# The order of the on-chip tensors in SBUF changed: operand tiles, weight homes, WORK and BIG first, landing buffers and residual behind

## What is computed

```python
for layer in range(2):                       # first block
    u = rmsnorm(h, norm_g[layer, 0])
    m = even_mixer(u, ...) if layer == 0 else nsa_mixer(u, ...)   # u @ w_in, attention-like work, @ w_out
    h = h + rmsnorm(m, norm_g[layer, 1])
    u = rmsnorm(h, norm_g[layer, 2])
    gate, up = split(u @ ffn_w_gu[layer])    # 2048 -> 2 x 5632
    h = h + rmsnorm((silu(gate) * up) @ ffn_w_down[layer], norm_g[layer, 3])
for layer in range(2):                       # second block, smaller mixers: 2048 -> 2048, 512 -> 2048, then a final rmsnorm
    ...
```

## The kernel before

| tensor | before | after |
|---|---|---|
| `H`, the residual | 16512 to 32896 | 198912 to 215296 |
| `UTH` | 32896 to 49280 | 16512 to 32896 |
| `UTL` | 49280 to 65664 | 32896 to 49280 |
| `RAW0` to `RAW3` | 65664 to 82048 | 182528 to 198912 |
| `WH`, `WL` of homes 0 to 2 | 82048 to 106624 | 49280 to 73856 |
| `BIG` | 106624 to 172288 | 116864 to 182528 |
| `WORK` | 172288 to 215296 | 73856 to 116864 |
| `HTH` (in `BIG`) | 106624 to 151680 | 116864 to 161920 |
| `HTL1` (in `BIG`) | 151680 to 163968 | 161920 to 174208 |
| `HTL0` (in `WORK`) | 172288 to 205056 | 73856 to 106624 |
| extra homes 0 to 3 (in `WORK`) | 172288 to 205056 | 73856 to 106624 |
| extra homes 4 and 5 (in `BIG`) | 127360 to 140416 and 168064 to 172160 (`XL5`) | 137600 to 150656 and 178304 to 182400 (`XL5`) |
| `WC`, `MK`, `ONE`, `SM` and the small ones | from 215296 | the same |

## Time and profile before

### The profile page before, as it was taken

How to read it: one execution, slowest core, us unless ns; L and a number is a source line. 1 busy time by engine, 2 the same in 40 slices (tenths; PEclk the granted TensorE clock), 3 DMA queues, 4 the chain that set the end, 5 groups by cost and what they waited for, 6 DMA issues and landing times.

```text
span 2812.7 us, 33205 instructions
## 1 busy us (share of the span) xinstructions
PE 2787.0 (99%) x13548; PEld 2320.3 (82%) x13548; DVE 1578.5 (56%) x2212; ACT 1368.8 (49%) x2031; POOL 61.0 (2%) x83
## 2 busy tenths in 40 slices
PE   9999999999999999999999999999999999999998
PEld 7788888888888888888888888888888888887777
DVE  6665777755545454444644555654555544466666
ACT  6645454545444444333634544644444443356565
POOL 0000000000000000000010000000000000000002
PEclk9999999999999999999999999999999999999999
DMA  7855544665666666555655434666666655565444
GB/s 233 139 128 131 108 105 99 167 208 178 193 182 193 189 190 190 188 194 187 218 172 155 135 105 153 191 189 193 187 190 185 194 188 191 190 204 170 153 142 135
DMA packets 213497, 481.12 MB, mean 171 GB/s; under 512 B 15584, under 2 KB 16352, under 8 KB 212704
## 3 DMA queue, kind: packets, MB, share of 16 engines
q1 hardware_dynamic: 210848, 467.78, 56.9%
q0 software_dynamic: 2352, 11.17, 1.1%
q10 hardware_dynamic: 144, 0.05, 0.0%
HBM read 476.84 MB, written 2.10 MB: 170 GB/s over the span
## 4 chain that ended last, share of the span: by engine, by line
PE 90%; DVE 5%; ACT 2%; DMA 1%; issue 1%; POOL 0%; SPq 0%; ACTq 0%; POOLq 0%
PE PS L1105 19%; PE PS L1107 19%; PE PS L1106 19%; PE PS L1154 8%; PE PS L1153 8%; PE PS L1152 8%; DVE WL L2150 1%; DVE WORK L2309 1%; PE PS L1366 1%; ACT WH L1628 1%; PE PS L1269 1%; PE PS L1486 1%; PE PS L1184 1%; PE PS L1281 1%; PE PS L1282 1%
## 5 line engine op out<-in xcount | busy, mean ns | idle before, releaser
L2150 DVE TENSOR_TENSOR WL<-RAW,WH 128x1024 fp32r<-128x1024 f32 x826 | 1011.0, 1225 | 940.8 <-ACT WH L1628 939.1
L1628 ACT ACTIVATE WH<-RAW 128x1024 fp32r<-128x1024 f32 x830 | 874.8, 1055 | 841.6 <-PE PS L1107 526.9
L1105 PE MATMUL PS<-WH,UTH 128*128 128x512 f32 x2396 | 955.9, 399 | 3.9 <-DVE WL L2150 3.0
L1107 PE MATMUL PS<-WH,UTL 128*128 128x512 f32 x2396 | 935.1, 390 | 0.0
L1106 PE MATMUL PS<-WL,UTH 128*128 128x512 f32 x2396 | 934.0, 390 | 0.0
L1105 PEld LDWEIGHTS PS<-WH,UTH 128*128 128x128 f32 x2396 | 450.2, 188 | 99.3 <-issue 4.0
L1107 PEld LDWEIGHTS PS<-WH,UTL 128*128 128x128 f32 x2396 | 449.8, 188 | 97.3
L1106 PEld LDWEIGHTS PS<-WL,UTH 128*128 128x128 f32 x2396 | 450.6, 188 | 87.1
L1154 PE MATMUL PS<-WH,HTL 128*128 128x512 f32 x656 | 259.3, 395 | 0.0
L1153 PE MATMUL PS<-WL,HTH 128*128 128x512 f32 x656 | 258.8, 394 | 0.0
L1152 PE MATMUL PS<-WH,HTH 128*128 128x512 f32 x656 | 255.4, 389 | 0.0
(11 more groups left out here) (421 smaller groups left out, 2413.4 us busy)
## 6 DMA issues: line engine op xcount, KB each, us to landing
RAW<-in_ffn_w_gu SPq DMA_DIRECT2D x352, 512.0 KB, 4.3
RAW<-in_ffn_w_down SPq DMA_DIRECT2D x176, 512.0 KB, 4.5
RAW<-in_ab_w_in SPq DMA_DIRECT2D x128, 512.0 KB, 4.7
RAW<-in_nsa_w_in SPq DMA_DIRECT2D x80, 512.0 KB, 3.7
RAW<-in_w_in SPq DMA_DIRECT2D x64, 512.0 KB, 4.0
RAW<-in_ab_w_out SPq DMA_DIRECT2D x32, 512.0 KB, 4.6
RAW<-in_nsa_w_out SPq DMA_DIRECT2D x32, 512.0 KB, 4.2
RAW<-in_w_out SPq DMA_DIRECT2D x16, 512.0 KB, 4.4
```

The costliest lines, as they stand in the source:

```text
L1105: e.matmul(o, lh, wh[:, j], start=k + j == 0, stop=False)
L1107: x = e.matmul(o, ll, wh[:, j], start=False, stop=k + j == NKT - 1)
L1628: e.activation(wh, raw, ACTF.Copy).then_inc(*a_hi.inc(s))
L2150: e.tensor_tensor(wl, raw, wh.bitcast(F32), ALU.subtract).then_inc(*v_lo.inc(s))
```

## The change

The declarations in `build` stand in another order. No instruction, size, semaphore or loop is touched, and every engine has the same instructions in the same order as before. What moves is where each tensor lies (the table above). `WORK` and `BIG` also change places, and what is laid over them goes along.

```diff
-        H = sb("H", 2 * D)[:].rearrange("p (t n) -> p t n", t=2)
         UTH = sb("UTH", NKT * 256, F32R)[:].rearrange("p (k n) -> p k n", k=NKT)
         UTL = sb("UTL", NKT * 256, F32R)[:].rearrange("p (k n) -> p k n", k=NKT)
-        RAW = [sb(f"RAW{i}", SLOT)[:] for i in range(NRAW)]
         WHL = [(sb(f"WH{i}", SLOT, F32R)[:], sb(f"WL{i}", SLOT, F32R)[:]) for i in range(NW)]
+        work_at = -(-nc.sbuf_base // 32) * 32
+        WORK = sb("WORK", 10752)[:]
         big_at = -(-nc.sbuf_base // 32) * 32
         BIG = sb("BIG", 2 * CHUNKS_EVEN)[:]
-        work_at = -(-nc.sbuf_base // 32) * 32
-        WORK = sb("WORK", 10752)[:]
+        RAW = [sb(f"RAW{i}", SLOT)[:] for i in range(NRAW)]
+        H = sb("H", 2 * D)[:].rearrange("p (t n) -> p t n", t=2)
         GB = WORK[:, 8704:10752]
         room = [work_at + 4096 * i for i in range(8)] + [big_at + 4 * a for a in (5184, 6400, 7424, 15360)]
```

## The result

The changed kernel takes 2806.99 us (median of 8 runs, 2806.17 to 2814.97). The ratio to the kernel before is 0.9966, with a 95% interval of 0.9955 to 0.9977: 0.34% faster, 0.9 us under the forecast. The profiled execution has a span of 2804.4 us where it had 2812.7, 8.3 us less. The 0.9 us under the forecast are mostly not in the trace: the forecast put 2.9 us around the span, taken from the span of one execution and the median of others, and the profiled execution of the changed kernel, whose own time is known, has 1.8 us (2806.17 less 2804.4).

The account below looks back on a forecast made before the run. TensorE was taken to bound the kernel, by matmul count times spacing. -6.8 - 1.6 + 0.4 + 0.3 = -7.7 us on a 2812.7 us span, plus 2.9 us around it, gave 2807.9 us; range 2806.6 to 2809.6, widened 2 us below and to 2813 above.

Parts of the forecast that it names:

- a costly region: From about byte 172200 of a partition up, TensorE's reads cost more: 6.2 ns a matmul (moving), 13.2 ns a triple (stationary).
- What bounds the kernel: TensorE, busy 99% of the span, sets the time: the number of matmuls times their spacing.
- `HTL0`, 6.8 us: Feed-forward stages: moving `HTL0` from byte 172288 to 73856 saves 13.2 ns in each of 512 triples, 6.8 us off.
- The extra homes, 1.6 us: Extra homes 0 to 3 move down too: 432 matmuls at up to 6.2 ns, bounds 0 to 2.7 us, 1.6 us off.
- The end of `HTL1`, +0.4 us: Tiles k = 42 and 43 of `HTL1` move past about byte 172200: 32 triples at 13.2 ns, 0.4 us lost.
- `XL5`, +0.3 us: `XL5`, moving operand of 32 matmuls, moves up to byte 178304: 6.2 to 13.2 ns each, 0.3 us lost.
- The rival of no change: The cost hangs on which tensors are read in turn and returns with new neighbours: 2815.6 us; chance 0.15 within 0.2%.
- The slower rival: The bottom of memory, where `UTH` now lies, costs like the top: 2816 triples, 37.2 us more, 2845 us; chance 0.07.
- Landings and the copies of ScalarE and VectorE, 0: Loads landing in high buffers, and `RAW` read from there by ScalarE and VectorE, cost nothing; later landings could cost 2.2 us.

Follow-up runs that it names:

- `before_work128`: The kernel before, in its old order, with 128 bytes of unused space ahead of `WORK`, which then starts at byte 172416; 2805.58 us, ratio 0.9969.

## Why the prediction was right, and where it was wrong

The time lay in the forecast range, but the mechanism that the forecast rests on, a costly region, does not exist.

**What bounds the kernel: right.** Nothing moved but the spacing of TensorE, and the span followed its busy time.

**`HTL0`, 6.8 us: right in size, not in cause.** 512 triples went from 693.2 to 680.0 ns, and the count from the starts gives 6.8 us.

**The extra homes, 1.6 us: slightly too much.** They gave 1.2 us. In the open stretch the gain was in full, 3.96 to 3.85 us over 17 spacings; behind transposes and waits it was covered, as supposed, and more of them may stand there than I took; that was not counted.

**The end of `HTL1`, +0.4 us, and `XL5`, +0.3 us: wrong, both are nothing.** The step that failed is the reading of the cause: "somewhere at about byte 172200 of a partition a region begins from which TensorE's reads cost more, whichever operand it is". The rows were right, and so was the grouping of tensors into slow and quick; the property that I picked to tell them apart was one of two that fit. The address splits them at 172200, and so does the remainder by 256. The runs put the second in its place: fp32r matmuls cost 6 to 7 ns more when their operands differ in that remainder, in either order of the tensors. I held against a relation between operands that like spacings came with very different distances. Those distances, such as 118784 bytes, are all multiples of 256, and the 65664 bytes from `HTH` to `HTL0` are 256 x 256.5. (The prediction counts five extra tensors with the low spacing; the extra homes 4 and 5 are four.)

That the time was hit all the same was luck of the case: region and remainder agree on every term but the two small ones, and the errors (0.7 us of loss that did not come, 0.4 us of gain that did not) nearly cancel. For the kernel `before_work128` the prediction's reasoning would have said no change, and it would have missed all of it.

**The rival of no change.** It said that the cost may hang on which tensors are read in turn. As a form of the cause it was nearer than my own; its consequence, a like cost among the new neighbours, did not come, since the move happened to make all fp32r operands alike. The Trainium skill, page "SBUF — State Buffer", section "Who interferes with whom", was the page for that rival; the runs contradict the reading of it by which a place costs TensorE nothing (2804.4 against 2841.1 us of span by 128 bytes of two tensors).

**The slower rival.** `UTH` at the bottom costs nothing. That 37.2 us, its price for slow triples on `UTH`, is close to what `UTH` and `UTL` cost when they are unlike (36.7 us) is chance: it is made of 13.2 ns a triple in all 2816 triples, while the run has some 20 ns a triple where nothing interrupts (3 x 6.6) and much of it covered elsewhere. The run that has 13.2 ns a triple, with `UTL` alone, costs 27.3 us.

**Landings and the copies of ScalarE and VectorE, 0: right.** TensorE's waits stayed at 6.5 and 6.6 us, and the busy times of both engines moved by 0.6 us or less.

What stays open: why the remainder by 256 bytes matters, differences under 32 bytes, other data types, and what keeps the spacing from settling with an unlike `WL`.

## What to carry to other kernels

Where TensorE streams fp32r matmuls back to back, lay all their operands, stationary and moving, at the same remainder by 256 bytes, tensors laid over others included; a single pad of 128 bytes was worth 0.3% here, and two tensors 128 bytes off cost 1.3% (36.7 us of 2804.4). When a step in the spacing follows a tensor, list every property in which it differs from its neighbours (region, remainder, distance, buffer) before naming one, and look for a tensor on which two of them disagree, or make one with a pad. A change of declarations that seems to be about order may work by its remainders alone.

## What the runs showed of the hardware

- **The remainder by 256 bytes.** On fp32r operands with 512 moving columns the spacing is 226.7 ns with like remainders (0, 128, 160 and 192 tried) and 233.3 ns with unlike ones (32, 64 and 128 apart), at a granted clock of 1.00 in both. One unlike stationary tile slows two matmuls. An unlike `WL`, moving in one of three, costs 6 to 7 ns a triple in some stretches and 20 ns in most. Transposes of 128 columns, and the one fp32 matmul that was seen both ways, show no difference (272 and 274 to 275 ns). The Trainium skill, page "SBUF — State Buffer", section "Operand start alignment", calls the start address a question of "legality, not speed" and says that its own runs timed nothing; here it is one of speed.
- **A fall of the granted clock.** In the kernel with all operands at 160, and in the one with `WL` alone, the clock fell once, for 13.7 us, and the time was some 7 us longer. Stretches of the first of these: from and to, us, PE busy (instructions), granted clock, DMA share, GB/s.

```profile
1404.00:1408.00 4.00, 3.13 (x19) 1.00 0.07 28
1408.00:1412.00 4.00, 4.00 (x29) 0.72 0.38 102
1412.00:1416.00 4.00, 4.00 (x21) 0.50 0.00 0
...
1420.00:1424.00 4.00, 4.00 (x12) 0.57 0.72 203
1424.00:1428.00 4.00, 4.00 (x21) 1.00 1.00 302
```

The same stretches of the kernel after:

```profile
1404.00:1408.00 4.00, 3.25 (x26) 1.00 0.07 7
1408.00:1412.00 4.00, 4.00 (x39) 1.00 0.32 96
1412.00:1416.00 4.00, 4.00 (x24) 1.00 0.08 9
```

0.50 is the lower level, 1.2 GHz. Ahead of the fall TensorE was idle for 0.9 us of 4 and then ran matmuls of 60 columns, among which the clock fell; the kernel after has nearly the same there (0.75 us idle) and kept its clock. The length of that idle time does not decide it: right ahead of the same matmuls it was 0.87 us in this kernel and 0.68 us in the one with `WL` alone, where the clock fell, and 0.74, 0.92 and 1.15 us in the kernel after, the one with the `WL` of home 0 and the one with all at 192, where it did not. So it comes to one execution and not to another. It is a likely source of the single runs some 7 us above the rest. Of the 8 runs of the changed kernel the one at 2814.97 us has a mean clock of 0.997, the other seven, 2806.17 to 2807.58 us, have 0.999. With all at 192 four of ten have 0.997 (2812.01 to 2814.47 us), the other six, 2807.05 to 2808.45 us, have 0.999. And among the 13 of the kernel before that stand beside the last kernels, those at 2821.12 and 2822.19 us have a mean clock of 0.997, and the other eleven, 2813.2 to 2815.61 us, have 0.999. For a difference of 8 us a single run therefore proves little; the spacing in the trace does not depend on it.
